# Four state-space groups on one core: gate values in two buffers, the next group's inputs ahead of the last group's normalisation

## What is computed

```python
def mamba2_branch(z, xBC, dt_raw, conv_w, conv_b, dt_bias, a_log, d_skip, ssm_norm):
    xBC = jax.nn.silu(causal_depthwise_conv(xBC, conv_w, conv_b)).astype(jnp.float32)
    gn = SSM_N_GROUPS * SSM_D_STATE
    xs = xBC[..., :SSM_D_INNER].reshape(b, S, SSM_N_HEADS, SSM_HEAD_DIM)
    Bm = xBC[..., SSM_D_INNER:SSM_D_INNER + gn].reshape(b, S, SSM_N_GROUPS, SSM_D_STATE)
    Cm = xBC[..., SSM_D_INNER + gn:].reshape(b, S, SSM_N_GROUPS, SSM_D_STATE)
    dt = jax.nn.softplus(dt_raw.astype(jnp.float32) + dt_bias.astype(jnp.float32))
    A = -jnp.exp(a_log.astype(jnp.float32))
    y = ssd_chunked(xs, dt, A, Bm, Cm) + d_skip.astype(jnp.float32)[:, None] * xs
    y = y.reshape(b, S, SSM_D_INNER) * jax.nn.silu(z.astype(jnp.float32))
    yg = y.reshape(b, S, SSM_N_GROUPS, SSM_D_INNER // SSM_N_GROUPS)
    yg = yg * lax.rsqrt(jnp.mean(yg * yg, axis=-1, keepdims=True) + EPS)
    y = yg.reshape(b, S, SSM_D_INNER) * ssm_norm.astype(jnp.float32)
    return y.astype(z.dtype)
```

## Time and profile before

| | |
|---|---|
| median of 3 runs | 2020.23 us (2019.01 to 2023.79) |
| profiled execution | 2019.28 us |
| its span, first to last instruction | 2017.4 us |
| busy share PE / PEld / POOL / ACT / DVE | 98% / 92% / 77% / 52% / 35% |
| mean granted clock of PE | 0.994 |
| the stretch 1395 to 1600 us (the four groups) | PE busy 184.73 of 205 us, DVE 133.86, POOL 124.61, ACT 116.49, granted clock 0.95 |

### The profile page before, as it was taken

The page is one execution under the profiler, slowest core; times in us unless marked ns, Lnnn a source line. Parts: engine busy times, 40 slices in busy tenths (PEclk is TensorE's granted clock), DMA queues, the critical chain, the costliest instruction groups (busy, mean ns, idle before and its releaser), DMA issues.

```text
span 2017.4 us, 34350 instructions
## 1 busy us (share of the span) xinstructions
PE 1969.3 (98%) x14430; PEld 1863.4 (92%) x14430; DVE 713.0 (35%) x1300; ACT 1045.9 (52%) x1345; POOL 1563.2 (77%) x1226
## 2 busy tenths in 40 slices
PE   7999999999999999999999999999888999999998
PEld 7999999988999999999999889998888999999997
DVE  1531856422100231056652220005665854022001
ACT  6434683456534554357544663347555566345333
POOL 7889786675988789878676579887565787789985
PEclk9999999999999999999999999999999999999999
DMA  8555543253555555554314445555323344455552
GB/s 316 177 195 182 189 147 105 81 179 138 188 188 188 194 207 191 184 201 147 128 61 147 162 174 186 188 196 185 126 85 125 126 150 146 165 188 181 187 187 103
DMA packets 48538, 332.60 MB, mean 165 GB/s; under 512 B 5376, under 2 KB 6272, under 8 KB 10112
## 3 DMA queue, kind: packets, MB, share of 16 engines
q1 hardware_dynamic: 43920, 314.60, 43.4%
q10 hardware_dynamic: 4464, 15.80, 2.3%
HBM read 329.33 MB, written 1.05 MB: 164 GB/s over the span
## 4 chain that ended last, share of the span: by engine, by line
PE 82%; DVE 7%; ACT 5%; DVEq 2%; POOL 1%; issue 1%; ACTq 1%; DMA 1%; SPq 0%
PE bank L1660 23%; PE bank L1661 23%; PE bank L1662 22%; ACT arena L371 2%; ACT whi L371 1%; PE bank L1773 1%; POOL wlo L350 1%; PE bank L2016 1%; PE bank L2032 1%; PE bank L1753 1%; PE bank L1755 1%; ACT L371 1%; DVE x L1002 1%; DVE arena L975 1%; DVE arena L1442 1%
## 5 line engine op out<-in xcount | busy, mean ns | idle before, releaser
L350 POOL TENSOR_TENSOR wlo<-raw,whi 128x512 fp32r<-128x512 f32 x1188 | 1521.9, 1319 | 397.5 <-ACT whi L371 397.4
L1660 PE MATMUL bank<-uT_hi,whi 128*128 128x256 f32 x2560 | 733.1, 286 | 2.1 <-DVE memT_lo L1038 2.1
L1661 PE MATMUL bank<-uT_lo,whi 128*128 128x256 f32 x2560 | 725.7, 283 | 0.0
L1662 PE MATMUL bank<-uT_hi,wlo 128*128 128x256 f32 x2560 | 725.7, 283 | 0.0
L371 ACT ACTIVATE whi<-raw 128x2048 fp32r<-128x2048 f32 x297 | 566.7, 1910 | 170.4 <-PE bank L1662 148.3
L1660 PEld LDWEIGHTS bank<-uT_hi,whi 128*128 128x128 f32 x2560 | 492.7, 192 | 6.5 <-DVE memT_lo L1038 2.4
L1661 PEld LDWEIGHTS bank<-uT_lo,whi 128*128 128x128 f32 x2560 | 492.8, 192 | 3.9 <-issue 2.0
L1662 PEld LDWEIGHTS bank<-uT_hi,wlo 128*128 128x128 f32 x2560 | 492.5, 192 | 0.0
L371 ACT ACTIVATE arena<-bank 128x512 f32<-128x512 f32 (+3 forms) x285 | 153.8, 554 | 343.6 <-PE bank L1662 263.5
L1050 DVE TENSOR_TENSOR bank<-arena,bank 128x512 f32<-128x512 f32 x50 | 34.8, 696 | 606.0 <-PE bank L1662 606.0
L1660 PE MATMUL bank<-whi,hT_hi 128*128 128x512 f32 x440 | 171.8, 390 | 0.0
(11 more groups left out here) (269 smaller groups left out, 2591.0 us busy)
## 6 DMA issues: line engine op xcount, KB each, us to landing
raw<-in_w SPq DMA_DIRECT2D x297, 1024.0 KB, 4.8
rows<-in_rows ACTq DMA_DIRECT2D x23, 512.0 KB, 4.9
arena<-in_mem ACTq DMA_DIRECT2D x2, 1024.0 KB, 7.2
x<-in_x SPq DMA_DIRECT2D x2, 512.0 KB, 6.4
out<-x SPq DMA_DIRECT2D x2, 512.0 KB, 2.7
arena<-in_amask ACTq DMA_DIRECT2D x1, 768.0 KB, 7.7
cst<-in_cst SPq DMA_DIRECT2D x1, 452.0 KB, 12.5
arena<-in_lvl SPq DMA_DIRECT2D x1, 384.0 KB, 13.7
```

The lines of the kernel that those rows point to most:

```text
L350: r = pool.tensor_tensor(wlo[n % LAND][:, k], raw[n % LAND][:, k], whi[n % RING][:, k].bitcast(F32), ALU.subtract)
L1660: pe.matmul(o, l[0], r[0], start=start, stop=False)
L1661: pe.matmul(o, l[0], r[1], start=False, stop=False)
L1662: return pe.matmul(o, l[1], r[0], start=False, stop=stop)
```

## The change

- `zg` becomes two buffers (the second at offset 10240 of the arena), used in turn by groups.
- ACT does `z_out` of group g+1 in the iteration of group g, around the second `conv_silu`; the roots of y of group g (`y_roots`) move into group g+1, behind the copies of x. In group 0 the two Exp of the decay columns go ahead of `conv_in(0, 1)`.
- DVE does the normalisation of group g in group g+1, behind `xdec`.
- In group 2 the 16 transposes of y go behind the first convolution unit, into banks 3, 6, 1, 7; `hi_parts` goes behind `conv_in`, `lo_parts` behind the normalisation.

```diff
-        zg = view(3096, NT, 512)
+        zg = [view((3096, 10240)[i], NT, 512) for i in range(2)]
...
             conv_in(0, 0)
-            conv_in(0, 1)
             act.wait_ge(sems["cs_cols"], p.count("cs_cols"))
             fn(gs[:, :, 96:128], gs[:, :, 64:96], AF.Exp)
             fn(gs[:, :, 128:160], gs[:, :, 128:160], AF.Exp).then_inc(sems["col_decay"], 1)
+            conv_in(0, 1)
             conv_silu(0, 0)
...
             for g in range(SSM_GROUPS):
-                if g == 0:
-                    conv_silu(0, 1)
-                else:
-                    z_out(g, 0)
-                    z_out(g, 1)
-                if g == 2:
-                    hi_parts(mT, (2, 3, 6, 4))
                 for c in range(2):
                     b = (1, 7)[c]
                     act.wait_ge(sems[f"act_bank{b}"], p.count(f"act_bank{b}"))
                     fn(xs[:, c, :], bank[b][:, :], AF.Copy).then_inc(sems["xs_out"], 1)
-
+                if g:
+                    y_roots(g - 1)
                 if g < SSM_GROUPS - 1:
                     conv_in(g + 1, 0)
...
+                if g == 2:
+                    hi_parts(mT, (3, 6, 1, 7))
...
                     conv_silu(g + 1, 0)
                     conv_in(g + 1, 2)
+                    z_out(g + 1, 0)
                     conv_silu(g + 1, 1)
+                    z_out(g + 1, 1)
...
                 tt(heads(xdec), heads(xdt[:, 0, :]), bc8(128, 0), ALU.mult).then_inc(sems["x_dt"], 1)
+                if g:
+                    normalise(g - 1)
+                if g == 2:
+                    lo_parts(mT, (3, 6, 1, 7))
...
-                if g == 2:
-                    transposes(ysb, (2, 3, 6, 4), "y_ready", (3, 1))
                 if g:
                     last_channels()
...
                 proj_T(conv_bank[0], "conv" if g < SSM_GROUPS - 1 else "dve", uT, False, None if g else last_channels)
+                if g == 2:
+                    transposes(ysb, (3, 6, 1, 7), "y_ready", (3, 1))
                 row_sums(0)
```

More of the change, by code:

```diff
@@ L804, in z_out @@
                 act.wait_ge(sems["unit_done"], u + 1)
-                fn(zg[:, :, j * 256:(j + 1) * 256], half2((z_bank if g else first_z_bank)[j]), AF.Silu)\
+                fn(zg[g % 2][:, :, j * 256:(j + 1) * 256], half2((z_bank if g else first_z_bank)[j]), AF.Silu)\
                     .then_inc(sems["tok_out"], 1)
@@ L820, in _, with y_roots @@
             fn(gs[:, :, 128:160], gs[:, :, 128:160], AF.Exp).then_inc(sems["col_decay"], 1)
+            conv_in(0, 1)
             conv_silu(0, 0)
             conv_in(0, 2)
-            for g in range(SSM_GROUPS):
-                if g == 0:
-                    conv_silu(0, 1)
-                else:
-                    z_out(g, 0)
-                    z_out(g, 1)
-                if g == 2:
-                    hi_parts(mT, (2, 3, 6, 4))
+            def y_roots(g):
+                for t in range(NT):
+                    act.wait_ge(sems["y_raw"], p.count("y_raw"))
+                    fn(junk2, ysb[:, t, (g % 2) * 512:(g % 2 + 1) * 512], AF.Square, accum_out=st[:, 10 + t:11 + t])
+                    root(st[:, 10 + t:11 + t], st[:, 10 + t:11 + t], 512).then_inc(sems["y_rms"], 1)
+            conv_silu(0, 1)
+            for g in range(SSM_GROUPS):
                 for c in range(2):
@@ L857, in _ @@
                     split_to(att0 + 3)
[L858 to L861, removed]
+            y_roots(SSM_GROUPS - 1)
             def swap(pr, j):
@@ L1445, in convolve, with columns, normalise @@
                     r.then_inc(sems["conv"], 1)
+            def columns(g):
+                return slice((g % 2) * 512, (g % 2 + 1) * 512)
+            y_row = [None]
+            def normalise(g):
+                if g % 2 == 0:
+                    y_row[0] = use_row()
+                yc, w = columns(g), y_row[0]
+                for c in range(2):
+                    dve.wait_ge(sems["y_rms"], p.count("y_rms"))
+                    dve.reciprocal(st[:, 10 + c:11 + c], st[:, 10 + c:11 + c])
+                    dve.drain()
+                    stt(ysb[:, c, yc], ysb[:, c, yc], st[:, 10 + c:11 + c], w[:, yc], ALU.mult, ALU.mult)\
+                        .then_inc(sems["y_ready"], 1)
             for g in range(SSM_GROUPS):
@@ L1461, in _ @@
                     convolve(0, 1)
-                if g == 2:
-                    lo_parts(mT, (2, 3, 6, 4))
                 dve.wait_ge(sems["dve_bank0"], p.count("dve_bank0"))
@@ L1506, in _ @@
                     convolve(g + 1, 1)
-                yc = slice((g % 2) * 512, (g % 2 + 1) * 512)
+                yc = columns(g)
                 dve.wait_ge(sems["tok_out"], p.count("tok_out", 2))
@@ L1514, in _ @@
                 for c in range(2):
[L1515 to L1523, removed]
+                    tt(ysb[:, c, yc], ytmp[:, c, :], zg[g % 2][:, c, :], ALU.mult).then_inc(sems["y_raw"], 1)
+            normalise(SSM_GROUPS - 1)
             dve.wait_ge(sems["amask_in"], p.count("amask_in", 16))
```

## The result

The changed kernel took 2001.68 us (median of 4 runs, 2001.08 to 2003.42), the kernel before 2021.28 us beside it on the same chip (the prediction started from 2020.23, the median of the first three of its four runs): ratio 0.9904, interval 0.9887 to 0.9921. It is faster, as forecast, but by less: 19.6 us in the medians, and 17.7 in the pair of profiled executions (2019.28 and 2001.61), where 24.8 was said. 2001.68 is 0.7 us above the top of the range. The span is 1999.7 us and the mean granted clock 0.998.

A forecast was written before the change was run, and what follows sets the result against it. PE, busy 98% of the span, was taken to bound the kernel; gains of 8.6 + 8.8 - 0.2 + 6.7 + 0.9 = 24.8 us from 2019.28 gave 1994.5, as a median of runs 1995.4, said as 1995, range 1992 to 2001.

The forecast's parts named there:

- The waits of groups 1 and 3: PE's waits for x_dt at the state product and the slow clock behind them go: 8.6 and 8.8 us, less 0.2.
- Group 0: Exp of the decay columns leaves the path to the first conv_silu: gain between 0 and 1.5 us, taken as 0.9.
- Group 2's new wait: Transposes of y wait for the moved normalisation: 2.3 to 3.7 us, taken as 2.5, plus 0.5 clock; gain 6.7 of 9.7.
- its own rule: A DVE tensor_tensor with both inputs in SBUF contends with POOL's reads: L1479 takes 1.59 us instead of 0.69.
- the first rival: POOL slows every step of x_dt and the normalisation: group 2's transposes 4.8 us late, 4.3 more in all, 1999; chance 0.17.
- The "cost nothing" for the moved normalisation: On DVE, 2.0 to 3.4 us of normalisation behind xdec is covered by PE's work before diagonal, so costs nothing.
- The sum: All gains together: 8.6 + 8.8 - 0.2 + 6.7 + 0.9 = 24.8 us.
- the 28.6 us of excess: PE's waits and slow-clock time in the four groups together, 28.6 us: the most that the change can give.
- Rival 2: ACT's split ahead of the copies of x waits for its raw unit: 6 us in all, 2001; chance 0.06.
- rival 3: The time comes back later: with POOL the limit behind the groups, PE waits there, 2020; chance 0.04.
- rival 4: Slower: ACT's second conv_silu and copies of x stand behind waiting gate copies; 10 us a group gives 2025; chance 0.03.
- the 0.1 a group: PE's wait at L2213 for ACT's second conv_silu, whose cover is only 0.2 us: taken as 0.1 us in a group.

The follow-up runs named there:

- Experiments 7: Changed kernel with the last group's normalisation behind DVE's rotations of queries and keys and its roots behind the first attention value_out: 2006.29 us, ratio 0.9917 to the kernel before.
- experiment 8: Changed kernel with the last group's roots behind ACT's six half copies and its normalisation just ahead of DVE's wait for the first attention result: 2001.90 us, ratio 0.9901.
- Experiment 1: Changed kernel with POOL writing zeros instead of subtracting in the 21 units around the groups: 1991.69 us, ratio 0.9846 to the kernel before.
- experiment 3: Changed kernel with x_dt's first step (L1493) reading x from PSUM instead of ACT's copy in SBUF: 1999.81 us, ratio 0.9887 to the kernel before.
- Experiment 2: Kernel before the change, with POOL writing zeros instead of subtracting in the same 21 units around the groups: 2009.85 us, ratio 0.9938.
- experiment 6: Changed kernel with group 2's y transposes behind the row sums and state product, and ACT's state copy ahead of hi_parts: 2001.69 us, ratio 0.9902.
- experiment 4: Changed kernel with the weight splits of the two gate units behind the roots of y instead of behind each gate copy: 2001.54 us, ratio 0.9894.

## Why the prediction was off

- **The waits of groups 1 and 3** (8.6 and 8.8 us less 0.2): right. Group 1 gave 8.58; in group 3 the row sums and the stretch behind them are back to 1.79 and 6.62 us. In group 1 the state product starts at T + 8.95 where T + 8.96 was said, and the clock behind it is not halved. The cover was thinner than it looked: x_dt ended at 1453.10, 0.17 us ahead of PE, because ACT's copies came 0.7 us sooner than summed and DVE's three products took 5.13 us instead of the 3.6 to 4.5.
- **Group 0** (0.9): 1.07 - 0.36 = 0.7. The size is luck. The wait of 1.25 is gone, as forecast, but the transposes that want the second `conv_silu` start only 0.71 us sooner than before (1408.94 and 1409.65); PE waits 0.71 there instead of 0.25, and the group itself is 0.36 longer. The 1.07 lie in the start, which varies by more.
- **Group 2's new wait** (2.5 us and 0.5 for the clock): this step failed. The mechanism, the place and the engine waited for were right; it measured 6.7, so group 2 gave 3.0 and not 6.7.
  - Two terms were too small. For L1479 the prediction took the middle between a quiet and a loaded row (0.69 and 1.59), though its own rule put POOL beside it in every group. For L1477 it took 1.43, the median of rows with POOL at work, and held that against the first rival. That median is no duration that occurs beside POOL: in group 1 of the kernel before the pair is 1.05 and 1.76, and 1.05 came about where the instruction began late in one of POOL's. In the changed kernel it began just behind the start of one, and the pair is 1.74 and 1.78. (Groups 2 and 3 have the same in both kernels.) From its own bounds of 2.3 to 3.7 it then took 2.5, below the middle. It also let POOL's row end at about T + 14 (three units); it was five units, to T + 28.5.
  - The first rival had the mechanism and said 4.8 and 1.5 for the clock, 6.3. That was the case to choose. Its durations were nearly right (the pair 3.42 against 3.54, L1495 1.60 against 1.59, L1463 1.53 against 1.48); its result came at T + 13.9 instead of T + 12.9 because the pair began at T + 5.4 in this group and not at T + 4.4. That the skip terms of group 1, stretched by POOL, make DVE and then ACT late in group 2 was in neither.
- **Nothing at all was said of the end of group 3**, whose 8.8 us were counted in full: this failed too. The "cost nothing" for the moved normalisation itself held: `diagonal` has no wait in the changed kernel, and DVE came to the skip terms of group 3 9.4 us sooner. But PE arrived at the scores 8.8 us sooner, and DVE's chain to the last rotation only 7.1 us. The skip terms of group 3, before and changed:

```profile
1576.48 1.28 DVE L1498 TENSOR_TENSOR arena<-arena,small 128x512 f32<-128x512 f32 x2
```

```profile
1554.74 3.48 DVE L1518 TENSOR_TENSOR arena<-arena,small 128x512 f32<-128x512 f32 x2
```

With L1522 at 1.00 (0.69 before) and the pair L1535 at 3.14 (2.40) that is 3.25 us more; 0.3 more goes to a wait for ACT, and 0.7 less to the normalisation behind and 0.5 less to the rotations. The scores wait 2.04 us (0.34 before), 1.7 lost, and 1.66 more at the low clock behind the wait. Experiments 7 and 8 show that the path is DVE's: 1.6 us to the scores come back when it has less ahead of the rotation, and in experiment 8 the 1.68 behind them too. Experiment 1 shows the cause: with POOL clearing the scores wait 0.3 us.
- **The sum**: 24.8 - 3.7 (group 2) - 1.7 (scores) - 1.7 (clock behind them) - 0.2 (group 0) = 17.5, and 17.7 was measured.
- **The cause behind both**: experiments 1 and 3 show that POOL's subtractions, by what they read, stretch DVE's instructions with two SBUF inputs. Experiment 2 shows that this is no cost of the change but one that both kernels pay. In the 28.6 us of excess some 10 were POOL's, and a like toll came back at the next places where DVE was late.
- Rival 2 did not come true: no split of a gate unit waited for its raw weights. Nor did rival 3 (nothing is lost behind the scores but the 1.66) or rival 4 (L2226 waits 1.3 us in four pieces, 0.7 in group 0 and 0.6 in group 2, against the 0.1 a group that the prediction took; in group 2 the wait for y covers it).
- Open: the clock behind the scores. Behind 2.0 to 2.1 us of waiting it fell to 0.50 to 0.66 in both traces of the changed kernel and in experiment 6, and stayed at 1.00 in experiment 3 behind the same 2.1 us, and in experiment 4 behind 2.9. So of the 4.6 us by which the stages of experiment 3 are shorter, 1.66 are this clock and not shown to come from its edit. What tells these apart no run here shows.

## What to carry to other kernels

When an edit moves transfers or casts earlier, list what the second engine does in the new overlap, and take each of its durations from rows that stand beside the same neighbour. An excess at a wait is not all yours when you remove the wait: take out of it what a shared resource costs, for that can come back at the next late place. Follow the gain to the next consumer of each in-order engine, beyond the loop in which the edit stands (here the attention scores behind the last group).

## What the runs showed of the hardware

- A product of DVE on 128x512 with two SBUF inputs takes 0.69 us alone and 1.60 beside POOL's subtractions, a pair 1.3 and 3.4 to 3.5. From PSUM the pair takes 1.29 with POOL at work. How long the first of a pair takes hangs on where in one of POOL's subtractions it begins (1.05 us late in one, 1.74 at the start of one). I had expected the slow rows from the trace before, but not that one such product could take 6.69 us (once, in experiment 4), until POOL's row had ended.
- POOL's clear of 128x512 takes 0.48 us (four in 1.93), its subtraction 1.3 us, and 1.7 where DVE takes turns with it. A clear beside it leaves DVE's pair at 1.29 us.
